# Issuing the constants on another queue and moving the hidden-state transposes: one change to a two-block network kernel

## The reference

```
h = rmsnorm(x, g)
x = x + 0.5 * (silu(h @ w1) * (h @ w3)) @ w2      # w1, w3: 1024 x 2816, w2: 2816 x 1024
h = rmsnorm(x, g_mix);  x = x + mix(h)            # block 1: Fourier, short convolution, pooling
h = rmsnorm(x, g)                                 # block 2: windowed attention, gated linear attention
x = x + 0.5 * (silu(h @ w1b) * (h @ w3b)) @ w2b
```

## Time and profile before

| | before |
|---|---|
| median of three runs | 2427.92 us |
| the profiled execution: its own time / its span | 2430.38 us / 2428.4 us |
| TensorE busy with matmuls | 2378.7 us (98%) |
| VectorE busy | 1339.0 us (55%) |
| ScalarE busy | 1184.1 us (49%) |
| DMA engines, mean share in the SyncE queue's packets | 52.3% |
| mean granted TensorE clock | 0.993 |
| chain that ended last: share of TensorE | 89% |

### The profile page before, as it was taken

How to read it: one execution, slowest core, us unless ns; L and a number is a source line. 1 busy time by engine, 2 the same in 40 slices (tenths; PEclk the granted TensorE clock), 3 DMA queues, 4 the chain that set the end, 5 groups by cost and what they waited for, 6 DMA issues and landing times.

```text
span 2428.4 us, 31240 instructions
## 1 busy us (share of the span) xinstructions
PE 2378.7 (98%) x10966; PEld 1941.7 (80%) x10966; DVE 1339.0 (55%) x1470; ACT 1184.1 (49%) x1270; POOL 0.2 (0%) x4
## 2 busy tenths in 40 slices
PE   7999999999999999998999999999999999999999
PEld 6887887887887787887788878788878887878887
DVE  4554566555555456554555566755455447576554
ACT  5444444545544344544544565455455446545543
POOL 0000000000000000000000000000000000000000
PEclk9999999999999999999999999999999999999999
DMA  6656355555556455665465542555555554335653
GB/s 193 191 181 219 131 192 181 189 186 173 179 185 216 142 170 173 190 191 181 143 189 193 179 156 87 157 170 177 194 171 181 191 193 161 100 124 172 190 178 134
DMA packets 311170, 419.14 MB, mean 173 GB/s; under 512 B 16990, under 2 KB 202086, under 8 KB 311048
## 3 DMA queue, kind: packets, MB, share of 16 engines
q1 hardware_dynamic: 306496, 409.13, 52.3%
q10 hardware_dynamic: 4552, 8.47, 1.0%
HBM read 416.50 MB, written 1.05 MB: 172 GB/s over the span
## 4 chain that ended last, share of the span: by engine, by line
PE 89%; DVE 3%; DMA 3%; ACT 2%; issue 2%; SPq 0%; ACTq 0%; DVEq 0%
PE psum L496 27%; PE psum L498 27%; PE psum L497 27%; PE psum L513 3%; DMA raw<-w_in_dram 1%; PE psum L745 1%; ACT whi L979 1%; DVE wlo L1402 1%; PE psum L758 1%; PE psum L586 1%; DMA raw<-w_conv_out_dram 0%; DMA raw<-w_b_dram 0%; PE psum L736 0%; PE psum L603 0%; SPq L375 0%
## 5 line engine op out<-in xcount | busy, mean ns | idle before, releaser
L1402 DVE TENSOR_TENSOR wlo<-raw,whi 128x2048 fp32r<-128x2048 f32 (+2 forms) x410 | 893.2, 2188 | 610.9 <-ACT whi L979 602.8
L979 ACT ACTIVATE whi<-raw 128x2048 fp32r<-128x2048 f32 (+2 forms) x411 | 748.6, 1832 | 515.3 <-DMA raw<-w_in_dram 106.8
L496 PE MATMUL psum<-whi,xt_hi 128*128 128x512 f32 (+1 forms) x2176 | 865.5, 398 | 9.4 <-DVEq L1431 5.9
L498 PE MATMUL psum<-whi,xt_lo 128*128 128x512 f32 (+1 forms) x2176 | 846.4, 389 | 0.0
L497 PE MATMUL psum<-wlo,xt_hi 128*128 128x512 f32 (+1 forms) x2176 | 844.6, 388 | 0.0
L496 PEld LDWEIGHTS psum<-whi,xt_hi 128*128 128x128 f32 x2176 | 412.4, 190 | 95.6 <-issue 17.6
L498 PEld LDWEIGHTS psum<-whi,xt_lo 128*128 128x128 f32 x2176 | 411.9, 189 | 85.6
L497 PEld LDWEIGHTS psum<-wlo,xt_hi 128*128 128x128 f32 x2176 | 412.9, 190 | 81.5 <-issue 2.9
L496 PE MATMUL psum<-whi,ht_hi 128*128 128x512 f32 x704 | 279.7, 397 | 0.0
L497 PE MATMUL psum<-wlo,ht_hi 128*128 128x512 f32 x704 | 278.3, 395 | 0.0
L498 PE MATMUL psum<-whi,ht_lo 128*128 128x512 f32 x704 | 278.2, 395 | 0.0
(11 more groups left out here) (225 smaller groups left out, 1474.3 us busy)
## 6 DMA issues: line engine op xcount, KB each, us to landing
raw<-w_in_dram SPq DMA_DIRECT2D x180, 512.0 KB, 4.5
raw<-w_a_dram SPq DMA_DIRECT2D x128, 512.0 KB, 4.8
raw<-w_b_dram SPq DMA_DIRECT2D x128, 512.0 KB, 4.8
raw<-ffn_w_gate_dram SPq DMA_DIRECT2D x88, 512.0 KB, 4.1
raw<-ffn_w_up_dram SPq DMA_DIRECT2D x88, 512.0 KB, 5.1
raw<-ffn_w_down_dram SPq DMA_DIRECT2D x80, 512.0 KB, 4.7
raw<-w_o_dram SPq DMA_DIRECT2D x16, 512.0 KB, 4.6
raw<-w_proj_b_dram SPq DMA_DIRECT2D x16, 512.0 KB, 4.7
```

The costliest lines, as they stand in the source:

```text
L496: nc.tensor.matmul(pair(p, m)[:, out], hi[:, c, t], whi[:, slot, w], start=first, stop=False)
L498: last = nc.tensor.matmul(pair(p, m)[:, out], lo[:, c, t], whi[:, slot, w], start=False, stop=final)
L979: nc.scalar.activation(whi[:, u % HL, 0:n], raw[:, u % RAW, 0:n], ACT.Copy).then_inc(hi_done, 1)
L1402: nc.vector.tensor_tensor(wlo[:, u % HL, 0:n], raw[:, u % RAW, 0:n], whi[:, u % HL, 0:n], ALU.subtract).then_inc(w_ready, 1)
```

## The change

Four edits. (1) The nine small constant DMAs are issued by SyncE, behind the two loads of x and ahead of the first weight unit, and no longer by ScalarE. (2) At the start ScalarE does `x_hi` before `split(0)`, VectorE `x_lo` before `split(0)`, and TensorE frees the weight slots after its transposes of x. (3) In the feed-forward loop TensorE transposes group g-1 after the first quarter of `wide`, not after the second. (4) In the same loop ScalarE and VectorE handle the transposed hidden state (`hidden_hi`, `hidden_lo`) between the two splits of a group, not after both.

```diff
@@ SyncE, start
+            eng.dma_start(ident[:, :], a["t_ident"]).then_inc(consts_in, 16)
+            for b in (1, 2):
...
+                    eng.dma_start(vrows[at:at + LAYERS * rows, b - 1, :], src).then_inc(consts_in, 16)
@@ TensorE, feed-forward loop
                         eng.wait_ge(hid_done, groups(e, f, g - 2, 2))
-                        wide(u0 + 2 * g, g % 2, XT, 0, 2)
+                        wide(u0 + 2 * g, g % 2, XT, 0, 1)
                         hidden_transposes(g - 1)
-                        wide(u0 + 2 * g, g % 2, XT, 2, 4)
+                        wide(u0 + 2 * g, g % 2, XT, 1, 4)
@@ TensorE, start
-            eng.sem_inc(w_used, HL)
             eng.wait_ge(consts_in, 16 * N_CONSTS)
...
             x_transposes("ffn0", 0)
+            eng.sem_inc(w_used, HL)
@@ ScalarE, feed-forward loop
                         split(u0 + 2 * g + 4)
+                        hidden_hi(g, bass.ds(e.it * 4 + 2 * g, 2))
                         split(u0 + 2 * g + 5)
-                        hidden_hi(g, bass.ds(e.it * 4 + 2 * g, 2))
@@ ScalarE, start (the nine dma_start are gone)
-            split(0)
             eng.wait_ge(done, e.after(done, ("v",)))
             x_hi("ffn0", 0)
-            for u in range(1, 3):
+            for u in range(3):
                 split(u)
@@ VectorE, feed-forward loop
                         split(u0 + 2 * g + 4)
+                        hidden_lo(g, bass.ds(e.it * 4 + 2 * g, 2))
                         split(u0 + 2 * g + 5)
-                        hidden_lo(g, bass.ds(e.it * 4 + 2 * g, 2))
@@ VectorE, start
-            split(0)
             x_lo("ffn0", 0)
             half_done()
-            split(1)
+            for u in range(2):
+                split(u)
```

More of the change, by code:

```diff
@@ L451, in _ @@
                 eng.dma_start(x[:, m, :], a["x"][0, m * P:(m + 1) * P, :]).then_inc(consts_in, 16)
+            eng.dma_start(ident[:, :], a["t_ident"]).then_inc(consts_in, 16)
+            for b in (1, 2):
+                at = 0
+                for name, rows in VEC_ROWS[b]:
+                    src = a[name].rearrange("l (c p) -> (l c) p", p=P) if len(a[name].shape) == 2 else \
+                        a[name].rearrange("l k (c p) -> (l k c) p", p=P)
+                    eng.dma_start(vrows[at:at + LAYERS * rows, b - 1, :], src).then_inc(consts_in, 16)
+                    at += LAYERS * rows
             with e.layers(1):
```

## The result

The changed kernel takes 2454.57 us in the median of four runs (2449.60 to 2455.72); four runs of the kernel before beside it have 2429.15 us. The ratio is 1.0098 with a 95% interval of 1.0081 to 1.0114: slower by some 24 us, where I had forecast 17.8 us and a range that ends at 2452. Three more executions took 2448.82, 2452.11 and 2453.52 us, so all seven have a median of 2453.52. The profiled execution has a span of 2447.7 us and is one of the two shortest of seven, so its trace alone understates the change. The direction and the place of the loss in the loop were forecast right; the size was not.

The account below looks back on a forecast made before the run. TensorE was taken as the bound, busy 2366.75 of 2401.80 us. Forty loop waits of 0.41 us (16.4 us) plus 1.4 us at the start gave 17.8 us on 2427.92: 2446 us, range 2440 to 2452.

Parts of the forecast that it names:

- the wait after a VectorE instruction ends 0.06 us behind it: Loop: TensorE's transposes start 0.06 us after `hid` ends, making the new wait 0.35 us per group with a table load.
- The restart term: Loop: transposes starting after a wait hold TensorE 0.06 us longer, since their first weight load lies bare.
- My upper bound: Loop: at most 0.47 us for each group with a table load, counting the restart cost twice; 19 us in all.
- the rival on the clock: Loop: waits drop TensorE's clock to half, 109 us more, 2555 us; much slower, including a dearer table load, had 0.06.
- The start is 1.4 us longer: Start: later weights delay `split(0)`, its raw slot, unit 2 and so the third quarter, from 26.2 to 27.5 us.
- My upper bound for the start: Start: constants landing at 10.6 us would end `x_hi` at 14.1 and the split at 18.3, +3.8 us.
- The comparison that I leaned on: Clock: it stayed 1.00 after the 2.5 us wait for `merged` near 925.15, so 0.35 us waits should not lower it.
- costed at nothing: Loop, edit 4: second split some 0.7 us later, covered by idle time of 4.18 us on ScalarE, 3.54 on VectorE.
- My lower bound of the start: Start: +0.7 us, half of 1.4; a gain was excluded because breaking even needed the constants to land at 6.8 us.
- the cost of the table load by the Trainium skill's page: Loop: the page's 2.66 us per switch would make the wait 1.79 us and the sum 72 us; left out.
- No change: Loop: the wait is absent because `hid` ends sooner or TensorE arrives later; 2429 us, chance 0.06.
- faster: Half-rate stretches of TensorE go away, giving back some 5 us; 2423 us if loop waits are absent, chance 0.02.

Follow-up runs that it names:

- e9: Edits 3 and 4 plus an early small silu at each turn's head, written into an existing tile, against the kernel before: 2430.53 against 2427.92 us, 1.0005.
- e6: Edits 3 and 4, but even groups' transposes back after the second quarter, odd ones early, against the kernel before: 2425.65 against 2426.36 us, 0.9998.
- e13: Edits 3 and 4 plus a small square root ahead of the silu in even groups, a second table load on the path: 2511.07 us in one execution.
- e7: Edits 3 and 4 with TensorE's two waits ahead of the transposes swapped, the one for `hid` last, against the kernel before: 2443.04 us, 1.0065.
- e3: Only the start changed (edits 1 and 2), against the kernel before: 2432.78 us, 1.0016 (1.0007 to 1.0025).
- e15: The start alone (edits 1 and 2), unaltered, profiled again: 2429.72 us in a single time, beside runs of the kernel before from 2427.93 to 2432.65.
- e2: Only edit 4, the order on ScalarE and VectorE, against the kernel before: 2430.14 us, 1.0009 (1.0000 to 1.0018).
- e11: The kernel before plus one unused tile of 64 bytes per partition in front of the parts' tiles, against the kernel before: 2431.36 us, 1.0008.
- e10: The kernel before plus one unused tile of 32 bytes per partition in front of the parts' tiles, against the kernel before: 2412.64 against 2427.92 us, 0.9937.
- e5: Edits 3 and 4 plus an early small silu at each turn's head, written into a new scrap tile, against the kernel before: 2413.03 against 2426.36 us, 0.9949.

## Why the prediction was wrong

**The loop: mechanism right, one term too small.** The 40 waits are there, only in the groups with a table load, and e9, e6 and e13 show by three ways that the late gates cause them. The step that failed is "the wait after a VectorE instruction ends 0.06 us behind it". I read that from a place with one wait; the transposes of `hid` stand behind two, and the second added 0.10 us (e7). The restart term of 0.06 us held (0.05). So a turn costs 0.50 us where I had 0.41, and a little less in other parts: from `hid` of group 0 to that of group 10 the delay against the kernel before grows by 149.90 - 145.99 - 1.28 = 2.6 us in the first part and by 2.2 us in the last (19.24 - 17.00), each over five waits. That is 0.48 us on average and 19 us in all, against 16.4. My upper bound, also 19, had just room for it.

**The start: the step that failed is the rival on the clock.** I applied it only to the waits of 0.35 us in the loop, and not to the one wait that I had myself made longer. "The start is 1.4 us longer" counted when the third quarter begins and stopped there: the 1.3 us measured confirm it. But the wait ahead of it grows from 0.5 to 3.5 us, since the quarter begins 1.3 us later and TensorE reaches it 1.7 us sooner, and with a wait of that length the clock falls in most executions; `hid` of group 0 is then some 4 us late (38.0 against 33.9). My upper bound for the start, 3.8 us, stood for late constants, not for this. How often the fall comes over many executions no run counts; e3's whole time says 4 us on the whole, with 1.7 to 6.1 possible.

The comparison that I leaned on, 2.5 us of waiting at 925 without a fall, was one case and no bound. The same trace, of the kernel before, has a shorter wait with a fall behind it, which I overlooked:

```profile
786.37 5.39 PE L586 MATMUL psum<-cs,tok 128*128 128x512 f32 x8 [1.90 <-ACT tok L1059]
```

```profile
786.80:790.20 3.40, 3.40 (x5) 1.33 (x4) 1.04 (x2) 2.28 (x2) 0.00 (x0) 0.50 0.48 124
```

The wait is 1.90 us long, and from 786.8 to 790.2 the granted clock is 0.50. The length of a wait alone does not decide it: 2.5 us in e15 were followed by a fall, 3.5 us in the changed kernel were not, nor was any of e13's 48 waits of up to 1.8 us. Why one is and another is not stays open.

**The sum.** 19 and 4 us give 23 of the measured 24. The range ended at 2452, and the median of 2454.57 is 8.6 us above my 2446: 2.6 us are the loop's, some 2.7 the start's, and 1.2 are no error of the sum, since the kernel before itself has 2429.15 us in its four runs and had 2427.92 in the three that I started from. The last 2 us are within the scatter. Taken on 2427.92 us, the ratio of 1.0098 would be 2451.7 us, just inside; so both terms were too small, but that the time fell outside hangs on 2 or 3 us.

**Edit 4.** It was costed at nothing. e2 has 1.0009 (up to 1.0018, 4 us), and e11 and e9, where nothing should differ, have 1.0008 and 1.0005. With no delay inside any part of e2's trace I read no cost into it.

**The others.** My lower bound of the start was argued wrongly: "to come out even, the constants would have to land at 6.8" forgets the weights, which by my own figure land at 11.6. The constants landed at 7.0, and the start was 1.3 us longer all the same. That `x_hi` ends at 11.6 as forecast comes from two misses that cancel, the constants 1.0 us sooner and the table load of 1.28 us that I had left in its old place. On the cost of the table load by the Trainium skill's page the rows were right to be preferred, and e13 says so again. *No change* and *faster* found nothing that speaks for them.

## What to carry to other kernels

Work moved ahead of its producer's usual end should be priced at its *late* case, and where a hardware loop has a table load at its head, every turn has that case; a tiny activation of the same function at the head of the body took the load off the path here (e9). When a change makes one wait of TensorE longer, ask what the clock does in it and behind it, not only how long it is, and read every fall in the trace before taking one wait as harmless. When the first function of ScalarE changes, its table load moves too. And look at the starts of like matmuls on different operands: if one operand has a slower pace, its address is a suspect that one unused tile can test.

## What the hardware showed unexpectedly

- The pace of the three-product matmuls depends on the address of the stationary operand. `ht` and the tiles of the mixing parts lay 32 bytes past a multiple of 64 in each partition, at 124512, `xt` on a multiple, at 106624. Steps are 0.2333 us with the former and 0.2275 us with the latter; on a multiple of 64, `ht` has 0.2270 us too (e10), and 32 bytes further it has 0.2333 again (e11). The pads moved other tiles too, but of what these matmuls read and write only `ht` was moved. That is 12 to 15 us of this kernel (e5, e10), more than any order of work won here.
- A second semaphore wait behind the one that is late costs about 0.1 us even when it is long fulfilled (e7). Put the late one last.
- TensorE's clock fell to half in or behind waits of 2.5 to 3.4 us at the start, in four of five executions, and stayed up behind one of 3.5 us; elsewhere it fell behind one of 1.9 us (the kernel before, 786.8 us).
